# The second mixer of a two-block layer written as one table of jobs, with its convolution accumulated in PSUM

## What is computed

```python
h = rmsnorm_2(x, mix_pre_norm[i])
u = h @ w_in[i]                       # 1024 -> 2*512 + 4*512
u_a, u_b = u[..., :c0], u[..., c0:c1] # then hq, hk, hv, hg, 512 wide each
y_conv = conformer_conv(u_a, u_b, conv_dw_w[i], conv_dw_b[i], conv_ln_w[i], conv_ln_b[i])
y_ret = retention_group(hq, hk, hv, hg)
y = jnp.concatenate([y_conv, y_ret], axis=-1) @ w_out[i]
x = x + rmsnorm_2(y, mix_post_norm[i])
```

## Time and profile before

| | us |
|---|---|
| median of 3 runs | 1923.91 (1922.42 to 1925.71) |
| the profiled execution | 1922.82 |
| its span, first to last instruction | 1920.9 |

### The profile page before, as it was taken

The page is one execution under the profiler, slowest core; times in us unless marked ns, Lnnn a source line. Parts: engine busy times, 40 slices in busy tenths (PEclk is TensorE's granted clock), DMA queues, the critical chain, the costliest instruction groups (busy, mean ns, idle before and its releaser), DMA issues.

```text
span 1920.9 us, 24210 instructions
## 1 busy us (share of the span) xinstructions
PE 1824.6 (95%) x8390; PEld 1434.5 (75%) x8390; DVE 870.9 (45%) x1677; ACT 749.2 (39%) x1204; POOL 773.4 (40%) x586
## 2 busy tenths in 40 slices
PE   6999999999999999899999999978888999999987
PEld 4777788888888887588888885755465888888865
DVE  5545554777764112521111228999736333320043
ACT  4444555655564222432222333222234333332242
POOL 3323344333334554244444442533131544544532
PEclk9999999999999999999999999989989999999998
DMA  5222243333324232233223331212011333333321
GB/s 175 77 79 60 73 121 110 99 99 98 105 85 139 91 99 88 88 110 92 99 95 98 97 96 48 88 44 66 22 56 44 101 98 98 94 103 104 105 66 44
DMA packets 46639, 170.49 MB, mean 89 GB/s; under 512 B 5184, under 2 KB 5312, under 8 KB 46304
## 3 DMA queue, kind: packets, MB, share of 16 engines
q1 hardware_dynamic: 43776, 156.77, 26.1%
q10 hardware_dynamic: 2784, 12.65, 1.9%
HBM read 167.24 MB, written 2.16 MB: 88 GB/s over the span
## 4 chain that ended last, share of the span: by engine, by line
PE 82%; DVE 12%; issue 3%; DVEq 1%; ACT 1%; DMA 0%; SPq 0%; POOLq 0%; POOL 0%; ACTq 0%
PE bank L340 25%; PE bank L342 24%; PE bank L341 24%; DVE cv_odd L1862 2%; DVE cv L1862 2%; DVE xs L1402 1%; PE bank L451 1%; PE bank L596 1%; DVE diag L1360 1%; PE bank L460 1%; PE bank L473 1%; PE bank L378 1%; DVE y_u L1405 1%; PE bank L388 1%; PE bank L600 1%
## 5 line engine op out<-in xcount | busy, mean ns | idle before, releaser
L314 POOL TENSOR_TENSOR w_lo<-raw,w_hi 128x512 fp32r<-128x512 f32 x578 | 766.6, 1347 | 1116.1 <-ACT w_hi L785 1115.9
L340 PE MATMUL bank<-u_hi,w_hi 128*128 128x512 f32 x1528 | 612.1, 401 | 12.2 <-DVE glu L1838 4.3
L342 PE MATMUL bank<-u_hi,w_lo 128*128 128x512 f32 x1528 | 596.4, 390 | 0.0
L341 PE MATMUL bank<-u_lo,w_hi 128*128 128x512 f32 x1528 | 595.9, 390 | 0.0
L785 ACT ACTIVATE w_hi<-raw 128x1024 fp32r<-128x1024 f32 x289 | 304.1, 1053 | 252.3 <-PE bank L342 249.9
L340 PEld LDWEIGHTS bank<-u_hi,w_hi 128*128 128x128 f32 x1528 | 287.8, 188 | 80.8 <-issue 18.0
L342 PEld LDWEIGHTS bank<-u_hi,w_lo 128*128 128x128 f32 x1528 | 287.5, 188 | 61.7
L341 PEld LDWEIGHTS bank<-u_lo,w_hi 128*128 128x128 f32 x1528 | 288.0, 189 | 60.7 <-issue 3.3
L340 PE MATMUL bank<-v_hi,w_hi 128*128 128x512 f32 x320 | 126.7, 396 | 0.6 <-ACT y_u L824 0.6
L342 PE MATMUL bank<-v_hi,w_lo 128*128 128x512 f32 x320 | 125.7, 393 | 0.0
L341 PE MATMUL bank<-v_lo,w_hi 128*128 128x512 f32 x320 | 124.7, 390 | 0.0
(11 more groups left out here) (274 smaller groups left out, 2258.5 us busy)
## 6 DMA issues: line engine op xcount, KB each, us to landing
raw<-weights SPq DMA_DIRECT2D x289, 512.0 KB, 3.6
bc<-acs ACTq DMA_DIRECT2D x16, 512.0 KB, 3.8
xs<-x SPq DMA_DIRECT2D x4, 512.0 KB, 5.2
xs<-x ACTq DMA_DIRECT2D x1, 2048.0 KB, 8.0
out<-xs SPq DMA_DIRECT2D x8, 256.0 KB, 2.0
rt<-ret_tables ACTq DMA_DIRECT2D x1, 1536.0 KB, 6.1
dist<-att_tables SPq DMA_DIRECT2D x1, 512.0 KB, 10.5
p_raw<-p ACTq DMA_DIRECT2D x1, 512.0 KB, 7.0
```

The source lines that it names most:

```text
L314: return nc.gpsimd.tensor_tensor(w_lo[:, slot, w], raw[:, slot, w], w_hi[:, slot, w].bitcast(F32), ALU.subtract)
L340: mm(dst, w_hi[:, slot, w], hi, start=first, stop=False)
L341: mm(dst, w_hi[:, slot, w], lo, start=False, stop=False)
L342: return mm(dst, w_lo[:, slot, w], hi, start=False, stop=last)
```

## The change

- **One table.** The phases `glu`, `retain` and `mix2_out` become one phase `mix2` with the order `MIX2_ORDER`; loops over heads are written out. The first three outputs of the out projection use banks 0, 1 and 3, and are run chunk by chunk (`out2_chunk`, `OUT2_CHUNKS`: heads 0 to 2, the convolution's four, head 3), put between the steps of the last head. The other five are whole units after it.
- **Taps.** ScalarE writes tap 0 to PSUM (`conv_seed`, bank 2 or 3 by chunk), VectorE adds taps 1 to 30 there in place (`taps`, order in `CONV_TAPS`: two chunks alternate, with stretches of one chunk between), ScalarE adds the bias and writes `cv` (`conv_out`). `cv_odd` and the additions are gone.
- **Norms.** The sums over features are one-column matmuls (`ret_sum`, `conv_squares`), the root's factor is corrected in 4 tiny steps (`row_factor`) and spread by 4 matmuls against the identity (`spread`); the diagonal steps are gone. The mean is subtracted straight from PSUM (`centre`).
- **Layer norm's end.** ScalarE takes the tanh and also the scaling by a half with the bias (`ln_biased`), then the root for the last head, then `v_hi`.
- **Scores.** Four pieces in three banks (4, 5, 7, 5), none of which waits for a reading.
- **rt.** Scaling the rotation tables moves ahead of the first `glu_scale`.

```diff
+MIX2_ORDER = [(part, n) for n in range(D_CONV // P) for part in ("a", "b")]
+MIX2_ORDER += [(part, h) for h in range(R_HEADS) for part in ("q2", "k2", "v2", "g2")]
+MIX2_ORDER += [("out2", c) for c in range(C8)]
+OUT2_BANKS = (0, 1, 3)
+OUT2_CHUNKS = (4, 5, 6, 0, 1, 2, 3, 7)
+
+CONV_TAPS = [(0, t) for t in range(1, 11)]
+CONV_TAPS += [tap for t in range(1, 21) for tap in ((0, t + 10), (1, t))]
...
+            def swaps(h):
+                if h:
+                    pe.wait_ge(sem("decayed"), 4 * h)
...
+            def out2_chunk(n):
+                c = OUT2_CHUNKS[n]
+                if c >= 4:
+                    pe.wait_ge(sem("ret_split"), c - 3)
+                else:
+                    pe.wait_ge(sem("conv_split"), c + 1)
+                for j in range(3):
+                    job = JOBS["out2", j]
...
+            for h in range(R_HEADS):
+                unit2(("q2", h))
+                if h:
+                    ret_scores(h - 1)
+                    values_turn(h - 1)
+                unit2(("k2", h))
+                if h:
+                    ret_values(h - 1)
+                unit2(("v2", h))
+                swaps(h)
+                if h == R_HEADS - 1:
+                    conv_mean()
+                if h:
+                    ret_sum(h - 1)
+                unit2(("g2", h))
+                if h:
+                    ret_spread(h - 1)
+            last_head = R_HEADS - 1
+            out2_chunk(0)
+            out2_chunk(1)
+            ret_scores(last_head)
+            values_turn(last_head)
+            conv_squares()
+            ret_values(last_head)
+            out2_chunk(2)
+            spread(2, ROW["ln"]).then_inc(sem("ln_rb"), 1)
+            ret_sum(last_head)
+            out2_chunk(3)
+            out2_chunk(4)
+            ret_spread(last_head)
+            for n in range(5, C8):
+                out2_chunk(n)
...
+            def conv_seed(c):
+                act.wait_ge(sem("cat_ready"), c + 1)
+                if c >= 2:
+                    act.wait_ge(sem("conv_done"), c - 1)
+                af(ps[2 + c % 2][:], cat31[:, c, 0:T], ACT.Identity, scale=conv_weight(c, 0)).then_inc(sem("conv_seeded"), 1)
...
+            for c in range(4):
                 act.wait_ge(sem("ln_scaled"), c + 1)
+                af(ln_t[:, c, :], cv[:, c, :], ACT.Tanh, scale=0.5, bias=half[:, c:c + 1]).then_inc(sem("ln_tanh"), 1)
+                act.wait_ge(sem("ln_tanh"), c + 1)
+                af(cv[:, c, :], cv[:, c, :], ACT.Identity, scale=0.5, bias=half[:, c:c + 1]).then_inc(sem("ln_biased"), 1)
+            row_root(ROW["ret", last_head])
+            for c in range(4):
+                act.wait_ge(sem("conv_silu"), c + 1)
+                af(v_hi[:, c, :], cv[:, c, :], ACT.Copy).then_inc(sem("conv_hi"), 1)
+            ret_high(last_head)
...
+            def taps(first, end):
+                for n in range(first, end):
+                    c, t = CONV_TAPS[n]
+                    if t == 1:
+                        dve.wait_ge(sem("conv_seeded"), c + 1)
+                    else:
+                        dve.wait_ge(sem("tap_done"), CONV_TAPS.index((c, t - 1)) + 1)
+                    at = VEC["conv31"] + c * (CONV31 + 1) + t
+                    stt(out=ps[2 + c % 2][:], in0=cat31[:, c, t:t + T], scalar=vec[:, at:at + 1], in1=ps[2 + c % 2][:],
+                        op0=ALU.mult, op1=ALU.add).then_inc(sem("tap_done"), 1)
...
+            taps(80, 82)
+            ret_gate(1)
+            row_factor(ROW["ret", 0])
+            taps(82, 84)
+            ret_norm(0)
+            taps(84, 86)
+            ret_rest(0)
+            decayed(1)
+            ret_silu(1)
+            taps(86, 100)
+            rotate(2)
```

More of the change, by code:

```diff
@@ L735, in _, with ret_sum, spread @@
-            retention(R_HEADS - 1, layer_norm)
+            def ret_sum(h):
+                pe.wait_ge(sem("ret_squared"), h + 1)
+                for t in range(QB):
+                    last = mm(ps[6][:, t:t + 1], sq[:, 0, t * P:(t + 1) * P], ones[:, 0:1], start=True, stop=True)
+                last.then_inc(sem("ret_summed"), 1)
+            def spread(bank, factor):
+                pe.wait_ge(sem("row_factor"), factor + 1)
+                for t in range(QB):
+                    last = mm(ps[bank][:, t * P:(t + 1) * P], tiny[:, 40 + t:41 + t].broadcast_to([P, P]), ident,
+                              start=True, stop=True)
+                return last
@@ new lines, in ret_spread, with conv_mean, conv_squares @@
+            def ret_spread(h):
+                spread(6, ROW["ret", h]).then_inc(sem("ret_rb"), 1)
+            def conv_mean():
+                for c in range(4):
+                    pe.wait_ge(sem("conv_done"), max(c + 1, 3))
+                    last = mm(ps[2][:], ones, cv[:, c, :], start=(c == 0), stop=(c == 3))
+                last.then_inc(sem("mean_sum"), 1)
+            def conv_squares():
+                for c in range(4):
+                    pe.wait_ge(sem("centred_squared"), c + 1)
+                    for t in range(QB):
+                        last = mm(ps[2][:, t:t + 1], ln_t[:, c, t * P:(t + 1) * P], ones[:, 0:1],
+                                  start=(c == 0 and t == 0), stop=(c == 3), skip_group_check=True)
+                last.then_inc(sem("ln_summed"), 1)
@@ L736, in _ @@
+            for c in range(3, C8):
+                job = JOBS["out2", c]
+                pe.wait_ge(lo_done, job.unit + 1)
+                pe.wait_ge(out_free[job.bank], job.m + (1 if job.bank < 2 else 0))
+                for t in range(TILES):
+                    last = exact(ps[job.bank][:], job.unit % RING, t, v_hi[:, t, :], v_lo[:, t, :], t == 0, t == TILES - 1)
+                last.then_inc(out_ready[job.bank], 1)
+            q, k = STATS["post2"]
+            stat_sum(q + C8)
             keep_clock(3)
-            outputs_and_norm("mix2_out", "post2", v_hi, v_lo, sem("y2_ready"))
+            stat_broadcast(k)
@@ new lines, in _ @@
+            decayed(0)
+            taps(66, 80)
+            rotate(1)
+            ret_var(0)
+            taps(80, 82)
[9 more added lines that the diff above has]
+            rotate(2)
+            ret_var(1)
+            taps(100, 102)
+            ret_gate(2)
+            row_factor(ROW["ret", 1])
@@ new lines, in _ @@
+            taps(102, 104)
+            ret_norm(1)
+            taps(104, 106)
+            ret_rest(1)
+            decayed(2)
+            ret_silu(2)
+            taps(106, len(CONV_TAPS))
+            rotate(3)
+            for c in range(4):
+                centre(c)
+            ret_var(2)
+            ret_gate(3)
+            row_factor(ROW["ret", 2])
+            ret_norm(2)
+            ret_rest(2)
+            decayed(3)
+            ret_silu(3)
+            dve.wait_ge(sem("ln_summed"), 1)
@@ L1992, in _ @@
+            row_var(ps[2][:, 0:QB], D_CONV)
+            row_factor(ROW["ln"])
+            for c in range(4):
+                ln_scale(c)
+            ret_var(3)
+            conv_silu(0)
+            conv_silu(1)
+            conv_rest(0)
+            conv_silu(2)
+            conv_rest(1)
+            row_factor(ROW["ret", 3])
+            conv_silu(3)
+            conv_rest(2)
             conv_rest(3)
[L1993 to L1994 removed]
+            ret_norm(3)
```

484 lines of the change are left out of this document (237 added, 247 removed).

## The result

The changed kernel takes 1891.48 us (median of three; 1890.83 to 1892.49), and 1891.45 in a second series (median of four; 1891.21 to 1891.63). A fourth execution of the first series took 5909.74 us at a granted clock of 1.00; nothing on record explains it, and it is left out of every figure here. The kernel before, run again beside the first series, took 1924.73 (median of four), so 33.2 us less; the ratio is 0.9827 (95% interval 0.981 to 0.9843). The forecast was 1882, with a range of 1869 to 1901: the sign and the range held, and of the 42 us forecast 33 came.

The account below looks back on a forecast made before the run. The second mixer was taken as bound by VectorE up to head 2, then by a chain of small steps; work 203.5, waits 18.9 and clock 2.5 made 224.9 us against 266.6, so 1882.2 us, range 1869 to 1901.

Parts of the forecast that it names:

- the waits left: TensorE's waits in the second mixer after the change: 18.9 us in all, the longest 8.7.
- the chain that takes the old one's place: Last head: layer norm's end on ScalarE, root, v_hi, then VectorE's v_lo; TensorE waits 8.7 us for it.
- Rival A: Second mixer's taps: PSUM taps somewhat dearer, 0.93 us each, 18 us reaching TensorE: 1900; beyond 1890, chance 0.15.
- C: Rival on the taps: an in-place step in one PSUM bank runs at half rate, 31 us slower, 1955; chance 0.04.
- 65 ns more for a PSUM source: VectorE's taps: the skill page's overhead, 7.8 us more and 1884 instead of 1882; the forecast took nothing.
- Rival D: Mixer not shortened: heads gain nothing, three out projection units (16.3 us) are all the cover: 1907; chance 0.05.
- Rival B: Last head's tail better covered: without v_hi queueing, 5 of 8.7 us, clock loss and some row_factor waits go: 1872; chance 0.12.
- the ledger: TensorE's time from the mixer's first unit after the pair to the out projection's last matmul: 224.9 us against 266.6.
- Clock: TensorE's lower clock in the last head, behind the wait for v_lo: 2.5 us.
- Work: TensorE's own work in the mixer: 203.5 us, from units 119.8, heads 31.4, layer norm 7.4, out projection 44.9.
- glu: GLU stage: TensorE waits 1.6 us for its bank behind glu_scale(1), after ten taps on one accumulator (9.3 us).
- The spreads: Three spreads wait for row_factor, queued behind the gate: 2.8, 2.1 and 2.2 us; its four tiny steps take 1.1.

Follow-up runs that it names:

- e6: Changed kernel with no chunk of the out projection beside the last head's chain, all eight chunks behind it: 1895.61 us.
- e5: Changed kernel with the taps accumulated in SBUF (cv) instead of PSUM, same order: 1911.49 us.
- e3: Changed kernel with row_factor ahead of the next head's gate and v_hi written between the tanh and bias pairs: 1874.37 us.
- e9: e7 with the out projection's second chunk moved between two halves of the layer norm's one-column squares: 1871.91 us.
- e4: Changed kernel with two float32 filler matmuls between unit g2 and the spread in heads 1 to 3: 1886.34 us.
- e7: e3 with four filler matmuls behind the last ret_sum, in the wait ahead of the fourth out chunk: 1875.18 us.
- e10: e5 with GpSimd's two subtractions per unit cut to 32 columns for the mixer's 24 units, leaving out part of the weights' low half: 1884.74 us.

## Why the prediction was right, and where it was off

**Right.** The bound (VectorE's taps beside GpSimd, then the tail's chain), the waits left, and the chain that takes the old one's place: 17.3 us of waits against 18.9 forecast. Rival A and C are gone with 120 taps between 739 and 756 ns and alternating taps starting 0.66 us apart: a PSUM accumulator costs VectorE nothing here. The 65 ns more for a PSUM source, an estimate from the Trainium skill's figures (VectorE: DVE Perf Modes, the TRN2 errata), aren't seen: 748 against the 743 of undisturbed SBUF taps. Rival D (the three units are all the gain there is) has fallen: e6 gives the moved chunks 4.2 us, and e5 gives the accumulators in PSUM 20.0. Those are parts taken away one at a time; what the other 9.0 of the 33.2 are (norms as one-column sums, scores in three banks, the order) I didn't separate. Rival B (v_hi and factor not queued) was priced at 1872; e3 does just that and takes 1874.4.

**Partly luck.** The time lies beyond 1890, where I had put rival A (0.15), D and C, and none of the three is what happened: the range held for another reason than the one that it was drawn for. And the miss is small because 1.6 us of waits too many stand against 8.6 us too few of work and clock.

**Off by 7.0 in the ledger: 231.9 against 224.9.** e9 gives the terms apart, since its last head has no slow stretch: its 214.2 less its waits (0.5 + 0.7 + 0.7 + 0.9) and the fill of 3.7 leave 207.7 us of work at the full clock. So the changed kernel's 231.9 are 207.7 of work, 17.3 of waits and 6.9 of clock.

- *Clock: 6.9, not 2.5.* This is the term that was mis-sized most. I priced the lower clock at one place, behind the longest wait, where it costs 2.1 (1377.99 to the last spread 6.52, in e9 4.40). The changed kernel pays it also behind a wait of 2.5: 1.6 in the second iteration (34.56 against 32.95) and 1.5 behind the third spread (6.64 from it to the scores, in e4 5.13); and 1.7 from the last values to the norm's spread (5.99, in e9 4.33). The prediction had the waits and did not ask what the clock does behind each. The second series' trace, 233.3 long with the same waits, has 8.3 of it.
- *Work: 207.7, not 203.5.* Most of this is a slip of arithmetic: a unit's first and last matmul start 1246.68 and 1252.03, and with the pitch of 0.23 that is 5.58 us, not the 5.45 that I wrote and used. Over 22 units it makes 2.9 us, and with it the forecast would have been 1885. Added up from start to start in e9, less the waits, 22 units take 122.8 (5.58 each), the small steps of four heads 32.1 (31.4 forecast), the layer norm 7.7 (7.4) and the out projection 45.1 (44.9). An iteration without waits is 30.40 us, as the scores of e7 show (rows below), where 29.7 had been put together.

```profile
1279.77 2.32 PE L722 MATMUL bank<-rot_q,rot_k 128*128 128x512 f32 x8
...
1310.17 2.10 PE L722 MATMUL bank<-rot_q,rot_k 128*128 128x512 f32 x7
```

- *Waits: 17.3, not 18.9.* glu 0.5 for 1.6: ten taps on one accumulator take 7.88, 0.79 each, not 0.93. In SBUF they do so too (e10: 7.92); so the accumulator's place doesn't explain the 0.93 of the earlier trace rows, and what does is open. The spreads came out near the forecast (7.5 for 7.1) through two errors that cancel: the four tiny steps take 1.8, one of them stretched to 1.07, where I had 1.1 in all, and I had allowed some 1.7 over the three heads for semaphores and for VectorE coming late, which was 0.1 a head.

Between the ledger (7.0, or 8.4 by the second series' 233.3) and the medians (41.7 forecast, 33.2 measured: 8.5) the rest is within the drift of single profiles. Behind the mixer nothing grew by more than 1 us: 470.3 us from the last matmul to the end, 469.4 before.

## What to carry over

When VectorE is the bound beside a busy GpSimd, look at how many of its operands lie in SBUF, not at the step's size: moving the accumulator to PSUM was worth 20 us, and small steps with two SBUF operands on the critical path are best put where GpSimd rests. A step that someone waits for goes ahead of the step that nobody waits for: three swapped lines brought more (12 us) than eight matmul chunks beside the chain (4 us). Price a wait of TensorE with the clock behind it: in this kernel 2.5 us of waiting cost another 1.5 or so in two places of three in one trace and in all three in the next. And add a term up twice before multiplying it by 22: 0.13 us a unit made 3 us.
